# A hybrid decoder step: memory attention does a prompt tile and a sequence in every step, ten steps in place of eighteen

## The reference, cut to what matters

```python
def mem_attend(q, mk, mv):
    s = jnp.einsum('nthd,nmhd->nhtm', q, mk).astype(jnp.float32) * (MEM_HEAD_DIM ** -0.5)
    p = jax.nn.softmax(s, axis=-1).astype(mv.dtype)
    return jnp.einsum('nhtm,nmhd->nthd', p, mv)
```

## Time and profile before

| | before |
|---|---|
| median of 3 runs | 2394.64 us |
| the profiled execution | 2392.62 us |
| span of its trace | 2391.0 us |
| attention stage in it, from the first key load to the last scaling | 907.6 to 1316.2 us |
| of that, memory attention | 907.6 to 1081 us |

### The profile page before, as it was taken

The page is one execution under the profiler, slowest core; times in us unless marked ns, Lnnn a source line. Parts: engine busy times, 40 slices in busy tenths (PEclk is TensorE's granted clock), DMA queues, the critical chain, the costliest instruction groups (busy, mean ns, idle before and its releaser), DMA issues. The chain is left out here.

```text
span 2391.0 us, 36475 instructions
## 1 busy us (share of the span) xinstructions
PE 2188.3 (92%) x14030; PEld 2014.0 (84%) x14030; DVE 1309.7 (55%) x1981; ACT 602.3 (25%) x1050; POOL 809.3 (34%) x591
## 2 busy tenths in 40 slices
PE   5969999999999996568779898999999999999997
PEld 5928887889999995455556898989999999999997
DVE  5078999999789996846764544331111121211123
ACT  4162222232242214203333212222111111111112
POOL 5103432222212214777763233443222322232221
PEclk9999999999999998757889999999999999999999
DMA  5003222233232346887763544211111111111112
GB/s 194 18 23 80 59 62 80 74 119 113 83 111 91 100 141 238 309 291 263 237 203 98 166 134 141 81 45 35 44 44 52 36 46 46 49 37 44 52 31 97
DMA packets 231681, 249.13 MB, mean 104 GB/s; under 512 B 37283, under 2 KB 192976, under 8 KB 228989
## 3 DMA queue, kind: packets, MB, share of 16 engines
q1 hardware_dynamic: 184974, 129.15, 17.8%
q0 software_dynamic: 23552, 70.28, 9.2%
q10 hardware_dynamic: 23031, 48.07, 5.4%
HBM read 212.37 MB, written 35.43 MB: 104 GB/s over the span
## 5 line engine op out<-in xcount | busy, mean ns | idle before, releaser
L419 POOL TENSOR_TENSOR ffn_w_lo<-ffn_w_raw,ffn_w_hi 128x1024 fp32r<-128x1024 f32 (+2 forms) x108 | 219.7, 2035 | 530.4 <-ACT ffn_w_hi L203 530.4
L397 PE MATMUL banks<-h_hi,in_w_hi 128*128 128x384 f32 (+1 forms) x1056 | 349.0, 331 | 7.2 <-PEq L1808 7.2
L399 PE MATMUL banks<-h_hi,in_w_lo 128*128 128x384 f32 (+1 forms) x1056 | 345.2, 327 | 0.0
L398 PE MATMUL banks<-h_lo,in_w_hi 128*128 128x384 f32 (+1 forms) x1056 | 344.8, 327 | 0.0
L397 PE MATMUL banks<-ffn_in_hi,ffn_w_hi 128*128 128x384 f32 (+1 forms) x1032 | 338.4, 328 | 5.3 <-POOL ffn_w_lo L419 3.8
L398 PE MATMUL banks<-ffn_in_lo,ffn_w_hi 128*128 128x384 f32 (+1 forms) x1032 | 338.1, 328 | 0.0
L399 PE MATMUL banks<-ffn_in_hi,ffn_w_lo 128*128 128x384 f32 (+1 forms) x1032 | 338.1, 328 | 0.0
L397 PE MATMUL banks<-halves,ffn_w_hi 128*128 128x384 f32 (+1 forms) x846 | 277.9, 328 | 18.2 <-DVE halves L2591 11.0
L399 PE MATMUL banks<-halves,ffn_w_lo 128*128 128x384 f32 (+1 forms) x846 | 277.6, 328 | 0.0
L398 PE MATMUL banks<-halves,ffn_w_hi 128*128 128x384 f32 (+1 forms) x846 | 277.5, 328 | 0.0
L419 POOL TENSOR_TENSOR in_w_lo<-in_w_raw,in_w_hi 128x1024 fp32r<-128x1024 f32 x48 | 127.4, 2657 | 386.8 <-ACT in_w_hi L203 386.8
(11 more groups left out here) (385 smaller groups left out, 3822.2 us busy)
## 6 DMA issues: line engine op xcount, KB each, us to landing
in_w_raw<-in_w_in SPq DMA_DIRECT2D x48, 512.0 KB, 3.7
ffn_w_raw<-in_w_ffn_in SPq DMA_DIRECT2D x44, 512.0 KB, 3.6
merge_gate<-gate_spill_dram SPq DMA_DIRECT2D x24, 544.0 KB
ffn_w_raw<-in_w_ffn_out SPq DMA_DIRECT2D x24, 384.0 KB, 3.4
gate_spill_dram<-second_out ACTq DMA_DIRECT2D x16, 544.0 KB, 2.7
room<-q_spill_dram ACTq DMA_DIRECT2D x8, 1024.0 KB, 7.3
q_spread<-q_spill_dram ACTq DMA_DIRECT2D x8, 1024.0 KB, 7.4
gate_spill_dram<-first_out ACTq DMA_DIRECT2D x8, 544.0 KB, 2.8
```

What stands on the lines that cost most here:

```text
L397: nc.tensor.matmul(out, self.w_hi[:, s, k, :], g.hi[:, k, a:a + w], start=(k == 0), stop=False)
L398: nc.tensor.matmul(out, self.w_hi[:, s, k, :], g.lo[:, k, a:a + w], start=False, stop=False)
L399: mm = nc.tensor.matmul(out, self.w_lo[:, s, k, :], g.hi[:, k, a:a + w], start=False, stop=(k == g.kc - 1))
L419: self.m.nc.gpsimd.tensor_tensor(self.w_lo[:, s, 0:g.kc, :], self.raw[:, s, 0:g.kc, :], self.w_hi[:, s, 0:g.kc, :], ALU.subtract).then_inc ...
```

## The change

`memory_attention` has 10 steps. Step i works on prompt tile i and on sequence i together. The scores of a prompt tile have banks 0 and 1, the turned keys banks 2 and 3; a sequence's scores go to bank 2 alone and VectorE adds them up in SBUF (`add_scores`). Keys have one slot in place of two, and one turned copy in place of two; values have four slots of their own. The set-up of the gather on VectorE (`dve_first`) stands behind the first tile's `invert` and `half_keys`. The ticks are dealt 31 and 50; in a step the first half of them stands ahead of the keys, the second half behind. Cut to the lists that set the order:

```diff
-    for i in range(QB + NSEQ + 2):
-        n = 0 if i < 3 else 3 if i < QB else 2
+    for n in (0, 1, 5, 5, 5, 4, 4, 3, 2, 2):
...
             def keys(s):
-                if s >= 2:
-                    sp.wait_ge(s_kT, s - 1)
-                sp.dma_start(ck[:, s % 2], ...).then_inc(ck_in[s % 2], 16)
+                if s:
+                    sp.wait_ge(s_kT, s)
+                sp.dma_start(raw, ...).then_inc(ck_in, 16)
...
             def keys_turned(s):
+                pe.wait_ge(ck_in, 16 * (s + 1))
+                if s:
+                    pe.wait_ge(s_sacc, s)
+                if s == 6:
+                    pe.wait_ge(s_sout, 1)
...
             def scores(i):
-                if i >= 2:
-                    pe.wait_ge(s_exp, i - 1)
+                if i:
+                    pe.wait_ge(s_exp, i)
...
+            def add_scores(s):
+                dve.wait_ge(s_ssc, s + 1)
+                got, into = m.B[2][:, 0:NMEM], sprob[:, s // 4, :]
+                if s % 4:
+                    dve.wait_ge(s_sacc, s)
+                    nc.vector.tensor_tensor(into, got, into, ALU.add).then_inc(s_sacc, 1)
+                else:
+                    nc.vector.tensor_copy(into, got).then_inc(s_sacc, 1)
...
+                if i < QB:
+                    scores(i)
+                if 1 <= i <= QB:
+                    turn(i - 1)
+                if i in (6, 9):
+                    sample_mix(i // 9)
+                for k in ticks[i][:half]:
+                    gather.pe_tick(pe, k)
+                if i < NSEQ:
+                    keys_turned(i)
+                if 1 <= i <= QB:
+                    mix(i - 1)
+                if i < NSEQ:
+                    sample_scores(i)
+                if i in (5, 8):
+                    sample_turn(i // 8)
+                for k in ticks[i][half:]:
+                    gather.pe_tick(pe, k)
...
                 if i < QB:
                     negmax(i)
+                if i in (4, 8):
+                    sample_negmax(i // 8)
+                for k in early[:1]:
                     gather.dve_tick(dve, k)
                 if 1 <= i <= QB:
                     half_turned(i - 1)
+                if i == 0:
                     pad_queries()
+                for k in early[1:]:
+                    gather.dve_tick(dve, k)
+                if i < QB:
+                    invert(i)
+                if i in (4, 8):
+                    sample_normalise(i // 8)
+                if i < NSEQ:
+                    half_keys(i)
+                if i == 0:
+                    gather.dve_first(dve)
+                for k in late[:1]:
+                    gather.dve_tick(dve, k)
+                if i < NSEQ:
+                    add_scores(i)
+                for k in late[1:]:
                     gather.dve_tick(dve, k)
```

More of the change, by code:

```diff
@@ L916, in memory_attention @@
     NG = NSEQ // 4
-    steps = QB + NSEQ + 2
+    steps = QB + 2
     with ExitStack() as ctx:
@@ L920, in memory_attention @@
         cv = ctx.enter_context(nc.sbuf_tensor("memc_v", [P, 2, 2, 512], F32))
-        ckT = [[mkvT[:, 4 + 2 * g:6 + 2 * g, :] for g in range(2)],
-               [mkv[:, g, 0:512].rearrange("p (h n) -> p h n", h=2) for g in range(2)]]
+        raw, ckT = ck[:, 0], ck[:, 1].rearrange("p a (h n) -> p (a h) n", h=2)
         prob = ctx.enter_context(nc.sbuf_tensor("mem_prob", [P, 2, MH, NMEM], F32))
@@ L926, in memory_attention @@
         total = ctx.enter_context(nc.sbuf_tensor("mem_total", [P, 2, 4], F32))
-        sprob = ctx.enter_context(nc.sbuf_tensor("mem_sprob", [P, NMEM], F32))
+        sprob = ctx.enter_context(nc.sbuf_tensor("mem_sprob", [P, NG, NMEM], F32))
+        stop = ctx.enter_context(nc.sbuf_tensor("mem_snegtop", [P, NG], F32))
+        stotal = ctx.enter_context(nc.sbuf_tensor("mem_stotal", [P, NG], F32))
         spT = ctx.enter_context(nc.sbuf_tensor("mem_sprobT", [P, 2, P], F32))
-        values = [cv[:, 0], cv[:, 1]] + [prob[:, k].rearrange("p h n -> p (h n)").rearrange("p (t n) -> p t n", t=2)
-                                         for k in range(2)]
+        values = [cv[:, 0], cv[:, 1], mkvT[:, 4:8, :].rearrange("p (t h) n -> p t (h n)", t=2), mkv[:, :, 0:512]]
         qpad = m.room[:, R_C + 4 * NT:R_C + 4 * NT + NSEQ * MH * 32].rearrange("p (s h n) -> p s h n", s=NSEQ, h=MH)
-        ck_in = [m.sem(f"memc_k_in{i}") for i in range(2)]
+        ck_in = m.sem("memc_k_in")
         cv_in = [m.sem(f"memc_v_in{i}") for i in range(4)]
@@ L952, in load_values @@
                     sp.wait_ge(s_spv, s - 3)
-                elif s >= 2:
-                    sp.wait_ge(s_pT, QB - 3 + s)
+                if s == 3:
+                    sp.wait_ge(m.mkv_stored, 32)
                 sp.dma_start(values[s % 4], m.cache_mem_v[s].rearrange("(t p) n -> p t n", p=P)
                              ).then_inc(cv_in[s % 4], 16)
-            for s in range(2):
+            for s in range(4):
                 keys(s)
-            for s in range(2):
                 load_values(s)
-            for s in range(2, NSEQ):
+            for s in (4, 5, 6):
                 keys(s)
[L964 to L967, removed]
+            load_values(4)
+            load_values(5)
+            keys(7)
+            load_values(6)
+            load_values(7)
         def gpsimd(pool):
@@ L1052, in tensor @@
             for i in range(steps):
-                if i in (13, 17):
-                    sample_turn((i - 13) // 4)
+                half = len(ticks[i]) // 2
                 if i < QB:
                     scores(i)
-                if QB - 1 <= i < QB + NSEQ - 1:
-                    keys_turned(i - QB + 1)
                 if 1 <= i <= QB:
                     turn(i - 1)
[L1061 to L1067, removed]
+                if i in (6, 9):
[11 more added lines that the diff above has]
+                for k in ticks[i][half:]:
                     gather.pe_tick(pe, k)
@@ L1118, in sample_normalise @@
                 dve.wait_ge(s_sexp, g + 1)
-                nc.vector.reciprocal(total[:, 0, g:g + 1], total[:, 0, g:g + 1]).then_inc(s_sinv, 1)
+                nc.vector.reciprocal(stotal[:, g:g + 1], stotal[:, g:g + 1]).then_inc(s_sinv, 1)
                 dve.wait_ge(s_sinv, g + 1)
-                nc.vector.tensor_scalar(sprob[:, :], sprob[:, :], total[:, 0, g:g + 1], None, ALU.mult
+                nc.vector.tensor_scalar(sprob[:, g, :], sprob[:, g, :], stotal[:, g:g + 1], None, ALU.mult
                                         ).then_inc(s_snorm, 1)
             for i in range(steps):
-                if 1 <= i <= QB:
-                    invert(i - 1)
+                half = len(ticks[i]) // 2
+                early, late = ticks[i][:half], ticks[i][half:]
                 if i < QB:
                     negmax(i)
[L1129 to L1135, removed]
+                if i in (4, 8):
+                    sample_negmax(i // 8)
+                for k in early[:1]:
                     gather.dve_tick(dve, k)
@@ L1166, in half_keys @@
                 act.wait_ge(s_kT, s + 1)
[L1167 to L1172, removed]
+                if s:
+                    act.wait_ge(s_ssc, s)
+                nc.scalar.copy(ckT[:, 0:2, :], m.B[2][:, :].rearrange("p (h n) -> p h n", h=2)).then_inc(s_kTe[0], 1)
             def half_turned(i):
@@ L1187, in sample_weigh @@
                 act.wait_ge(s_sneg, g + 1)
[L1188 to L1191, removed]
+                nc.scalar.activation(sprob[:, g, :], sprob[:, g, :], ACT.Exp, bias=stop[:, g:g + 1],
+                                     accum_out=stotal[:, g:g + 1]).then_inc(s_sexp, 1)
             def sample_turned(g):
@@ L1202, in sample_out @@
                 nc.scalar.copy(m.omT[:, 0:MH, SEQ + 32 * g:SEQ + 32 * g + 32],
-                               m.B[6][:, g * P:(g + 1) * P].rearrange("p (h n) -> p h n", h=MH)).then_inc(s_out, 1)
+                               m.B[3][:, 2 * P:3 * P].rearrange("p (h n) -> p h n", h=MH)).then_inc(s_sout, 1)
             gather.act_first(act)
             for i in range(steps):
-                if 1 <= i <= QB:
-                    normalise(i - 1)
+                half = len(ticks[i]) // 2
                 if i < QB:
                     weigh(i)
[L1211 to L1214, removed]
+                if i in (4, 8):
+                    sample_weigh(i // 8)
                 if 1 <= i <= QB:
                     half_turned(i - 1)
[L1217 to L1223, removed]
-                    gather.act_tick(act, k)
-        return Parts(sync, gpsimd, tensor, scalar, vector), (s_out, QB + NG)
+                if i in (6, 9):
+                    sample_out(i // 9)
+                for k in ticks[i][:half]:
+                    gather.act_tick(act, k)
+                if i < NSEQ:
+                    half_keys(i)
+                if i < QB:
+                    normalise(i)
+                if 1 <= i <= QB:
+                    out(i - 1)
+                if i in (5, 8):
```

(8 more changed lines are left out.)

52 lines of the change are left out of this document (17 added, 35 removed).

## The result

The change is slower: 2404.82 us, the median of 6 runs (2399.56 to 2408.04), against 2394.97 for the kernel before (6 runs, 2393.65 to 2397.87). The ratio on record is 1.0036, 95% interval 1.0026 to 1.0046, in which the quotient of the two medians, 1.0041, lies as well. The profiled execution took 2405.40 us, its span is 2403.8. In the two traces the last scaling of the attention stage ends at 1327.83 in place of 1316.19, 11.6 us later; of that, 1.5 us stand ahead of the stage (POOL's first fetch is at 909.83 in place of 908.38), and what comes behind it takes the same within 1.2 us (2403.8 - 1327.83 against 2391.0 - 1316.19). So the loss lies in the stage of the change.

What follows compares the result with a forecast made beforehand. POOL's fetch list was taken to set the pace from the first summed key to about 1247. 0 (first tick) + 1 (step 26) = +1 us on 2392.62, median 2.0 above: 2395.5 us; range 2382 to 2407.

Steps and rivals of the forecast that it cites:

- Rival 3: Key loads in the memory part: one slot is too few, a 10.1 us landing ends each step; 2406 us, chance 0.04.
- Rival 4: Memory part: the ten steps take as long as the eighteen, prompt attention has four ticks more; 2405 us, chance 0.04.
- First tick: Start of the memory part: first product at 933.1 against 933.47, nothing won; tick 1 at 939.4, 3 us late.
- Tick 15: Memory steps 2 to 4, up to where VectorE holds POOL back: 4 us late (3 to 6).
- Packed scores: Eight new `add_scores` on VectorE in the memory part: 0.35 us each, 2.8 us in all, at most 5.5.
- Steps 5 to 9: Memory steps with ticks 16 to 30, POOL limits; prompt attention's first row maximum at 1074.8, 9.7 us sooner (8 to 14).
- Hand-over: Ticks 31 to 34 move into prompt steps: POOL waits 5.2 us at key 36, 4.5 at key 37, 13.7 behind.
- Around 1159: POOL's wait for VectorE there, 2.26 us, falls away in prompt attention, leaving POOL 11.5 us late (4 to 16).
- The end: Prompt steps 24 to 26: value 46 at 1243.5, first maximum of step 26 at 1258 (1249 to 1265), against 1257.36.
- Rival 1: No stall at the hand-over: prompt attention keeps 8 us of head start, step 26 at about 1249.5; 2386.6 us, chance 0.32.
- Rival 2: POOL stays behind in prompt attention: 16 us late, a group's end adds 2; +7, 2402 us, chance 0.22.

Runs made afterwards that it cites:

- the ticks two a step: Kernel after the change with only ticks 62 to 70 dealt otherwise, two a step as the kernel before had them: 2400.08 us, ratio 1.0018.
- all three moves: Kernel after the change with ticks 31 to 35 sooner, ticks 62 to 70 two a step and the second `sample_mix` in memory step 8: 2391.42 us.
- tick 1 sooner: Tick 1 dealt to memory step 1 in place of 2: 2387.26 us on top of all three moves, 2401.46 us alone on the kernel after the change.
- the product in step 8: Kernel after the change with the second `sample_mix` moved from memory step 9 to step 8, ahead of tick 28: 2397.91 us, ratio 1.0011.

## Why the prediction was right or wrong

The range, 2382 to 2407, holds the time. The forecast, no change that can be told, did not come, and its own range of 2390.5 to 2400 does not hold it. That the wide range does is in part luck: its upper end stands on rivals 3 and 4 (2406 and 2405), whose signs did not show, and of the 11.7 us that steps 25 and 26 lose the prediction has 3.5 (10.5 in place of 7), and no rival has more. The stall at the hand-over came by the mechanism that the prediction describes. By the steps:

- *First tick*: 933.1 forecast, 932.65 measured; tick 1 939.4 and 939.80. Right. Tick 15 came at 981.39, 2.2 us late, where 4 (3 to 6) were forecast.
- *Packed scores*: 0.35 us each taken, between 0.35 and 0.69. The six adds take 0.415 us. The trace of before has a nearer row than the one halved, VectorE's copy of 128x256 out of PSUM (L2416), which takes 0.42.

```profile
L1094 DVE TENSOR_TENSOR mem_sprob<-banks,mem_sprob x6: 414/415/425, 936.4 to 1035.2; 128x256 f32<-128x256 f32 x6
```

- *Steps 5 to 9*: the first row maximum 1074.8, measured 1075.12. The sum is right, with luck in its terms. Value 13 comes 2 us late (1055.2 forecast, 1057.26 measured), and what follows the second `sample_mix` takes 3.0 us where 4.8 were taken. That call was put at 13.9 us and took 14.1 (7.00 + 3.56 + 3.56). But the rows of 11.9 and 13.9 us are not the two calls: each sums one source of values over both calls. In the trace of before the calls take 11.7 and 13.8 us (1030.83 to 1042.56, 1066.85 to 1080.67), by chance nearly the same.
- *Hand-over*: tick 31 was to end at 1080.3 and did at 1080.8. Key 37 was to wait 4.5 and waited 4.56. Key 36 was to wait 5.2 and waited 9.26: the prediction let POOL arrive 4 us late, but it had made up for that (key 35 is fetched 1.0 us later than before). POOL ended 14 us behind, as the 13.7 had it, by a longer wait after a smaller lag.
- *Around 1159* the old wait was to fall away. It did not: 2.67 us at 1176.45, where 2.26 stood. So 13.9 us were left at value 46, not 11.5.
- *The end, the step that failed*: "4 us to the first", then 10.5 to the next first maximum, 1258. The first part held (1245.88 + 4 = 1249.94). The second is 15.4 us, and step 26 took 10.3 where the old 7 were assumed. The prediction lists the right work, three ticks in one step, and prices it at 13 us up to TensorE's part of tick 64, but sums with 4 + 10.5 = 14.5 and gives no reason. Read from value 46, the 13 held: that part ended at 1259.62, 13.7 us behind it. Then only 1.5 us are left for the transposes, mask products and scores that TensorE still does ahead of the next first maximum. They took 3.3 us before (1254.10 to 1257.36) and 5.7 here (1259.62 to 1265.32). What the prediction had nothing for is what the list does to TensorE: it waits 4.22 us for VectorE, and the granted clock falls behind the wait. With the ticks two a step, the same step took 9.0 us.
- *Rival 1* was called the only sure gain. The head start was there, 9.4 us, and was spent by step 25. Its condition, no stall at keys 36 and 37, is first met by the kernel with all three moves, whose group's end is mended as well; with tick 1 sooner that one takes 2387.26, and rival 1 had 2386.6.
- *Rival 2* named its deciding point as 15 us at value 46. It came at 13.9, so by its own sign rival 2 did not come. Its 2402 is near for another reason: the first maximum of step 26 comes at 1265.32, where it had 1264.5, but 19.4 us behind value 46 in place of 14.5. The 2 us that it gives to a group's end are for another group, ahead of value 46.
- *Rival 3, one slot of keys.* What TensorE had waited for at the transposition of the keys (L982) after the change, and from the tile view of the keys its line on landing:

```profile
its engine sat idle before it (us, times) until:
  issue: 2.7, 4
  DVE mem_sprob L1096: 1.7, 1
...
DMA to landing us min/median/max: 3.4/6.0/8.3
```

  The transposition waited for no transfer: the rows name VectorE and "issue", in which the profile shows no wait. Loads landed in 3.4 to 8.3 us, and 9.3 us or more lie between the end of one transposition and the start of the next (929.97 and 939.26 are the nearest). The rule of the Trainium skill (Trainium Kernel Development and Optimization, Best Practices) to double-buffer does not bind here by this trace; a second slot was not tried.
- *Rival 4* needed a start at 1084. It was 1075.

## What to carry to other kernels

Where a queue works down a fixed list with a few slots, look for the consumer that frees each slot and ask when that consumer runs after the change: a stage that is shortened by ten us gains nothing if the list has to stand ten us for a consumer that moved behind it. Deal out interleaved work against the times at which the queue wants it, not in proportion to step lengths. And don't put a chain of a producer and its consumer on another engine into one step: one step apart it costs 0.35 us here, in the same step 4.2 and the clock behind it.

## What the runs showed of the hardware

The wait of 4.22 us at tick 64 is followed by products at 1.70 us in place of 0.92, and by a granted clock of 0.73 in a window that reads 1.00 without the wait; 4.25 us ahead of tick 64 did the same with the product in step 8. So the two levels, 2.4 and 1.2 GHz, are both met in this stretch, and the wait costs more than its length: the same work from tick 64 to the next first maximum takes 6.9 us behind it and 4.1 in the kernel before. The Trainium skill (TensorE: Matmul & The Clock Gate, Part 1) says that the array's clock goes by how busy it has been, at half rate after idleness; these rows agree. POOL's own pace did not move: where it waits for nothing, a fetch starts 1.25 us behind the one before it, in the median of each of the ten kernels.
